# Page loads of the index stage issued in the projection, two key pads placed a stage earlier, and a fifth page slot in the diagonal stage

## What is computed

```
x = layernorm(alpha * x + 0.5 * swiglu(x, ffn1))
a_q, i_q, i_w, q_lat, q_pe, dsa_row, mla_row = project(x)      # row: 64 key, 64 value, 32 index key
# branch A ("dsa"): an index score chooses the 256 best keys (132 for the prompt)
score = sum_h i_w[h] * relu(i_q[h] . k_idx)                    # over the cached keys too
o_a   = softmax(where(chosen, a_q . k / 8, -inf)) @ v
# branch B ("mla"): all keys, through a latent
o_lat = softmax((q_lat . c_kv + q_pe . k_pe) * scale) @ c_kv
x = layernorm(alpha * x + merge(o_a, o_lat) @ w_o)
x = layernorm(alpha * x + 0.5 * swiglu(x, ffn2))
```

## Time and profile before

| | us |
|---|---|
| median of 3 runs | 3232.73 |
| lowest and highest of them | 3229.4, 3234.01 |
| profiled execution | 3235.45 |
| its span, first to last instruction | 3233.7 |
| TensorE busy | 2981.4 (92%) |
| VectorE, ScalarE, GpSimd busy | 1415.6, 1001.1, 641.2 |

### The profile page before, as it was taken

The page is one execution under the profiler, slowest core; times in us unless marked ns, Lnnn a source line. Parts: engine busy times, 40 slices in busy tenths (PEclk is TensorE's granted clock), DMA queues, the critical chain, the costliest instruction groups (busy, mean ns, idle before and its releaser), DMA issues. The chain is left out here.

```text
span 3233.7 us, 45582 instructions
## 1 busy us (share of the span) xinstructions
PE 2981.4 (92%) x18298; PEld 2554.9 (79%) x18298; DVE 1415.6 (44%) x2116; ACT 1001.1 (31%) x1612; POOL 641.2 (20%) x562
## 2 busy tenths in 40 slices
PE   7999999778898889999999999996888988999997
PEld 7999879655576679998799997784656666999975
DVE  2222264468763352222532223644877444322236
ACT  2121233444442232212321222334444433211223
POOL 1111031221122141110221110411302132311103
PEclk9999999889898999999999999997999989999998
DMA  4222452300122332223432224513001233222243
GB/s 117 83 78 78 139 162 63 130 1 1 66 84 95 111 98 78 78 84 131 156 87 83 78 91 144 157 33 131 1 17 66 84 111 129 74 80 82 87 142 126
DMA packets 241737, 293.79 MB, mean 91 GB/s; under 512 B 12624, under 2 KB 205488, under 8 KB 235456
## 3 DMA queue, kind: packets, MB, share of 16 engines
q1 hardware_dynamic: 234688, 229.00, 23.0%
q0 software_dynamic: 6912, 62.92, 5.3%
HBM read 287.72 MB, written 3.88 MB: 90 GB/s over the span
## 5 line engine op out<-in xcount | busy, mean ns | idle before, releaser
L159 DVE TENSOR_TENSOR wlo<-raw,whi 128x1024 fp32r<-128x1024 f32 (+2 forms) x398 | 514.6, 1294 | 1295.4 <-ACT whi L153 1294.3
L153 ACT ACTIVATE whi<-raw 128x1024 fp32r<-128x1024 f32 (+2 forms) x398 | 418.5, 1053 | 1435.7 <-PE ps L608 864.6
L608 PE MATMUL ps<-xth,whi 128*128 128x296 f32 x2624 | 752.1, 299 | 5.4 <-PEq L770 5.4
L608 PE MATMUL ps<-xtl,whi 128*128 128x296 f32 x2624 | 754.6, 300 | 0.0
L608 PE MATMUL ps<-xth,wlo 128*128 128x296 f32 x2624 | 571.7, 300 | 0.0
L608 PEld LDWEIGHTS ps<-xth,whi 128*128 128x128 f32 x2624 | 494.6, 188 | 5.5 <-issue 5.5
L608 PEld LDWEIGHTS ps<-xtl,whi 128*128 128x128 f32 x2624 | 493.3, 188 | 0.0
L608 PEld LDWEIGHTS ps<-xth,wlo 128*128 128x128 f32 x2624 | 427.5, 188 | 0.0
L166 PE MATMUL ps<-whi,hth 128*128 128x512 f32 (+1 forms) x880 | 350.6, 398 | 10.0 <-DVE wlo L159 8.4
L168 PE MATMUL ps<-whi,htl 128*128 128x512 f32 (+1 forms) x880 | 346.9, 394 | 0.0
L167 PE MATMUL ps<-wlo,hth 128*128 128x512 f32 (+1 forms) x880 | 346.8, 394 | 0.0
(11 more groups left out here) (402 smaller groups left out, 4423.2 us busy)
## 6 DMA issues: line engine op xcount, KB each, us to landing
raw<-in_ffn_w_in SPq DMA_DIRECT2D x176, 512.0 KB, 3.8
raw<-in_ffn_w_out SPq DMA_DIRECT2D x176, 512.0 KB, 3.5
raw<-in_w_o SPq DMA_DIRECT2D x32, 512.0 KB, 3.3
raw<-in_w_in SPq DMA_DIRECT2D x16, 507.0 KB, 3.9
gb<-in_ln_g SPq DMA_DIRECT2D x6, 512.0 KB, 5.4
gb<-in_ln_b SPq DMA_DIRECT2D x6, 512.0 KB, 6.3
raw<-in_w_in SPq DMA_DIRECT2D x8, 338.0 KB, 3.9
x<-in_x_prompt SPq DMA_DIRECT2D x1, 1536.0 KB, 10.8
```

Of the source, the lines that this page charges most:

```text
L153: e.activation(dst, T.raw[:, s, 0:width], ACT.Copy).then_inc(S.hi_done, 1)
L159: e.tensor_tensor(w_lo, T.raw[:, s, 0:width], w_hi.bitcast(F32), ALU.subtract).then_inc(S.split_done, 1)
L608: mm = e.matmul(bank(u, up)[:, h, :], part[:, s, w], xp[:, k, o], start=(k == 0 and part is T.whi and xp is T.xth), stop=(k == KD - 1 and ...
```

## The change

Three things are moved or added. *First*, the first two page sets of the index stage are issued in the projection: their places are now fixed where the rounded weights lay (`hi_at`) and behind the keys in `xth`, and GpSimd issues them behind the wait for the last weight, ahead of the `sB` casts. In the index stage `high(0)` and `low(0)` come ahead of the new tokens' relu and score. *Second*, pads 0 and 1 of the prompt stage are cleared and filled at the index stage, by GpSimd at its start and by ScalarE behind its last relu; the prompt stage clears two pads, and TensorE's wait for `pe_keys` is gone. The score at the end of the index stage is copied in halves, bank 4 by VectorE and bank 5 by ScalarE. *Third*, the diagonal stage has a fifth place for a page set, where the score lay; the sets use places 0, 1, 2, 3, 4, 0, 1, 2. Set 4 is issued behind `low(1)` once the bias is set, set `r` from 5 on when the values of request `r - 5` have been used, and `low` trails by one. In that stage ScalarE runs `high(2p + 2)` in slot 4. The latent stage keeps its order. The diff, cut:

```diff
 # proj_tensors
+    T.pads = [... f"pkeys{i}" at T.score_at + 2 * HKEYS * 4 + i * PROMPT * 4 for i in range(2)]
+    T.pg4 = T.M.put("pg4", [P, PAGES, ROW], F32, T.score_at)
+    T.ip1_at = T.xth_at + 3 * PAST * 4
+    T.ip = [T.M.put(f"ip{i}", [P, PAGES, ROW], F32, at) for i, at in enumerate((T.hi_at, T.ip1_at))]
 # proj_stage, gpsimd
                 e.memset(q[:, :, :].bitcast(F32), 0.0).then_inc(S.stack_zero, 1)
+            e.wait_ge(S.w_used, B + NW)
+            for r in range(2):
+                page_load(e, T, r, T.ip[r][:, :, :], W["cache_dsa"], r)
             e.wait_ge(S.sa_done, 2)
 # prompt_block, gpsimd / tensor / scalar / vector
-            for pad in pads:
+            for pad in pads[2:4]:
                 e.memset(pad[:, :], 0.0).then_inc(S.pads_zero, 1)
...
-                    if i == 0:
-                        e.wait_ge(S.pe_keys, 4)
...
-            e.wait_ge(S.pads_zero, 2)
-            for pad, rows in ((pe_keys[0], slice(32, 64)), (pe_keys[1], slice(96, 128))):
-                for dst, src in pad_copy(pad, T.kcT, rows):
-                    e.activation(dst, src, ACT.Copy).then_inc(S.pe_keys, 1)
...
-            e.wait_ge(S.pads_zero, 4)
+            e.wait_ge(S.pads_zero, 2)
...
-            e.wait_ge(S.pe_keys, 4)
             e.wait_ge(S.key_step, 4)
 # page slots
+SLOTS = [[r % 2 for r in range(DEC_B)], [r % 4 for r in range(DEC_B)], [0, 1, 2, 3, 4, 0, 1, 2]]
 # index_block
+    def score_out(e, half, copy):
+        h = PAGES // 2
+        copy(T.score[:, 0:HPAST].rearrange("t (p i) -> t i p", i=PAGES)[:, half * h:(half + 1) * h],
+             T.ps[:, 4 + half, :].rearrange("t (i p) -> t i p", i=h))
 # index_block, gpsimd
-            for r in range(DEC_B):
-                if r >= 2:
-                    e.wait_ge(S.kl_done, r - 1)
+            for pad in pads[0:2]:
+                e.memset(pad[:, :], 0.0).then_inc(S.pads_zero, 1)
+            for r in range(2, DEC_B):
+                e.wait_ge(S.kl_done, r - 1)
                 page_load(e, T, r, ip[r % 2][:, :, :], cache_dsa, r % 2)
 # index_block, scalar
+            high(0)
             e.wait_ge(S.new_dots, 1)
             e.activation(new_relu..., ACT.Relu).then_inc(S.new_relu, 1)
-            high(0)
             high(1)
...
+            e.wait_ge(S.pads_zero, 2)
+            for pad, rows in ((pads[0], slice(32, 64)), (pads[1], slice(96, 128))):
+                for to, of in pad_copy(pad, T.kcT, rows):
+                    e.activation(to, of, ACT.Copy)
+            e.wait_ge(S.weighed, DEC_B // 2)
+            score_out(e, 1, cp)
 # index_block, vector
+            low(0)
             e.wait_ge(S.new_weighed, 1)
...
-            low(0)
             low(1)
...
-            e.tensor_copy(T.score[:, 0:HPAST]..., flat[:, 4 * 512:4 * 512 + HPAST]...)
+            score_out(e, 0, e.tensor_copy)
 # sample_block
+    slots = [T.pg[:, i, :, :] for i in range(4)]
+    if not M:
+        slots.append(T.pg4[:, :, :])
+    pg = [slots[i] for i in SLOTS[1 if M else 2]]
 # sample_block, gpsimd
-            for r in range(1, 4):
-                low(r)
-            for r in range(4, DEC_B):
-                values_done(r // 2 - 2, r % 2)
-                page_load(e, T, r, pg[:, r % 4, :, :], cache, r % 4)
-                low(r)
+            low(1)
+            if not M:
+                e.wait_ge(S.bias_set, 4)
+                pages(4)
+            low(2)
+            low(3)
+            if M:
...
+            else:
+                for r in range(5, DEC_B):
+                    values_done((r - 5) // 2, (r - 5) % 2)
+                    pages(r)
+                    low(r - 1)
+                low(DEC_B - 1)
 # sample_block, scalar
-                    if p + 1 < PAIRS and j == 6:
+                    if p + 1 < PAIRS and j == (6 if M else 4):
                         high(2 * p + 2)
```

More of the change, by code:

```diff
@@ L881, in proj_tensors @@
     T.score_at = A.top + 16384
+    T.pads = [T.M.put(f"pkeys{i}", [P, PROMPT], F32, T.score_at + 2 * HKEYS * 4 + i * PROMPT * 4) for i in range(2)]
+    T.pg4 = T.M.put("pg4", [P, PAGES, ROW], F32, T.score_at)
+    assert T.score_at + PAGES * ROW * 4 <= T.arena + 2 * KF * TOK * 4
     T.sI = T.M.put("sI", [SAMPLE, IH, P], F32R, A.top + 16384)
@@ L1471, in sample_step, with pad_copy @@
         e.match_replace(T.swork[:, :], best, left[:, :], TAKEN).then_inc(S.s_round_done, 1)
+def pad_copy(pad, src, rows):
+    return [(pad[rows, c:c + w], src[rows, k0:k0 + w]) for c, k0, w in ((0, 0, S0), (S0, TAIL, PROMPT - S0))]
 def prompt_block(nc, T, S, next_cache):
@@ L1940, with pages_there @@
 INDEX_SEMS = ["w_zero", "w_set", "kh_done", "kl_done", "turned", "out_act", "out_dve", "dots_done", "relu_done", "weighed",
[L1941 to L1956, removed]
+              "new_dots", "new_relu", "new_weighed", "scored", "pads_zero"]
+PAGE_SEMS = ["page_in0", "page_in1", "page_in2", "page_in3", "page_in4"]
+SLOTS = [[r % 2 for r in range(DEC_B)], [r % 4 for r in range(DEC_B)], [0, 1, 2, 3, 4, 0, 1, 2]]
+def pages_there(e, T, l, stage, r):
+    slot = SLOTS[stage][r]
+    a_layer = sum(slots.count(slot) for slots in SLOTS)
+    before = sum(slots.count(slot) for slots in SLOTS[:stage]) + SLOTS[stage][:r].count(slot)
+    e.wait_ge(T.page_in[slot], l * (16 * a_layer) + 16 * (before + 1))
 def page_load(e, T, r, dst, cache, slot):
@@ L2059, in high @@
             def high(r):
-                pages_there(e, T, l, 0, r % 2, r // 2)
+                pages_there(e, T, l, 0, r)
                 if r >= 2:
@@ L2253, in values_done, with pages @@
                 e.wait_ge(S.v_done, 10 * p + 5 * b + 5)
+            def pages(r):
+                page_load(e, T, r, pg[r], cache, SLOTS[1 if M else 2][r])
             low(0)
             for r in range(1 if M else 2, 4):
-                page_load(e, T, r, pg[:, r, :, :], cache, r)
+                pages(r)
             if M:
@@ L2263, in _ @@
                                 base=0, pattern=[[1, P]], channel_multiplier=-1).then_inc(S.ones_set, 1)
-            for r in range(1, 4):
-                low(r)
-            for r in range(4, DEC_B):
-                values_done(r // 2 - 2, r % 2)
-                page_load(e, T, r, pg[:, r % 4, :, :], cache, r % 4)
-                low(r)
+            low(1)
[5 more added lines that the diff above has]
+            if M:
+                for r in range(4, DEC_B):
+                    values_done(r // 2 - 2, r % 2)
+                    pages(r)
+                    low(r)
+            else:
+                for r in range(5, DEC_B):
+                    values_done((r - 5) // 2, (r - 5) % 2)
+                    pages(r)
+                    low(r - 1)
+                low(DEC_B - 1)
             if M:
@@ L2281, in turn_chunk @@
                     if g == 0:
-                        pages_there(e, T, l, stage, r % 4, r // 4)
+                        pages_there(e, T, l, stage, r)
                     for k in range(4):
-                        mm = e.transpose(bank(("c", ch))[:, k * P:(k + 1) * P], pg[:, r % 4, 4 * g + k, 0:RL], T.ident[:, :])
+                        mm = e.transpose(bank(("c", ch))[:, k * P:(k + 1) * P], pg[r][:, 4 * g + k, 0:RL], T.ident[:, :])
                     mm.then_inc(S.bank_ps, 1)
```

25 lines of the change are left out of this document (10 added, 15 removed).

## The result

The changed kernel takes **3200.89 us** (3195.75 to 3201.28), the kernel before 3232.86 in the same rounds (3229.4 to 3234.01): a ratio of 0.9899 with a 95% interval of 0.9882 to 0.9916. That is 32.0 us less, where 28.5 were forecast. The time lies in the forecast's range of 3196 to 3213, between the forecast of 3204.2 and rival (a), 3198.

What follows compares the result with a forecast made beforehand. TensorE's idle time in the index and diagonal stages was taken as what the change can win: 12.8 + 1.8 + 1.9 + 12.0 = 28.5 us off 3232.73, so 3204.2 us, range 3196 to 3213.

Steps and rivals of the forecast that it cites:

- rival (a): Diagonal-stage boundaries: shorter idle keeps the clock up, up to 1 us more each, 6 in all, 3198 us; chance 15%.
- Part 1, projection: Projection: issuing page sets 0 and 1 there costs 0 us; at worst 0.1 us per layer is lost.
- Part 1, index stage: Index stage: pages already landed, first transpose and relu sooner; 6.8 us layer 1, 6.0 layer 2, 12.8 in all.
- rival (b): Index stage: page 3 late or `high(2)` waits, stall moves on; 3 to 4 us back per layer, 3211 us; 14%.
- the 599.3 of the sum: Index stage of layer 1: forecast start of the first transpose, instead of 605.25, 5.95 us earlier.
- signs of being wrong: Index stage: the sign meant is a wait for a page before `high(2)` or `high(3)` of over 2 us.
- Part 2: Index stage's end: score copy split over VectorE and ScalarE, 0.9 us per layer, 1.8; moved memsets and key copies hidden.
- Parts 2 and 3: Part 2, index stage's end: 1.8 us; Part 3, prompt stage's start, key copies after two memsets instead of four: 1.9 us.
- Part 4: Diagonal stage: fifth place and `high` at slot 4 end boundary waits; 8.5 us layer 1, 3.5 layer 2, 12.0 in all.
- t0: Diagonal stage: moment a pair's last score is out; forecast floor for the next pair's first score matmul is t0 + 2.3.
- (c): Dense stages: less rest lowers the granted clock; over 1.3% eats the gain, 2.5% gives 3260 us; chance 4%.
- (d): Index stage: early-loaded pages not landed, or issues wait for `sA`; fifth place alone left, 3217 us; chance 3%.

Runs made afterwards that it cites:

- the pair of kernels with and without the 14 transposes: Changed kernel with `high` back at slot 6 in the diagonal stage: 3212.4 us; plus 14 identity transposes in TensorE's stall at each of six boundaries: 3206.7 us.
- a third buffer: Changed kernel with three places for pages in the index stage: 3191.6 us (ratio 0.9873).
- the last two kernels: Three-places kernel plus 13 transposes before the last index weighing and 24 before the prompt's keys: 3189.0 us; plus 4 at the index stage's head: 3188.2 us.

## Why the prediction was right, and where it was off

- **Part 1, projection: cost nothing, as said.** The two issues run at 584.49 and 585.99 for 1.19 and 0.94 us, and the `sB` cast starts at 587.22 (before 587.40). The pages had landed by 594.2, before the block began. The rule of the Trainium skill on the shared port (SBUF — State Buffer, "SBUF: two separate sides") made no difference that these durations show.
- **Part 1, index stage: 11.7 us instead of 12.8.** From the stage's start to the first relu 5.3 us were gained in layer 1 and 5.6 in layer 2, and 0.8 more in layer 1 up to the last relu. Against the kernel with Part 1 undone it is 10.5 to 10.8. The term that was off is the landing of set 3: I took its old time of 7.7 us to the new place. But `high(1)` no longer waits for a page of its own, so sets 2 and 3 are issued 1.5 us apart instead of some 3, and share the DMA engines; set 3 took 9.5 and 8.1 us. This is rival (b) in part, at 1.1 us over both layers and not at 3 to 4 each. One of the prediction's own signs of being wrong did appear: `high(3)` waited 3.41 and 2.3 us for its page. The first transposes also came 0.4 us later than the 599.3 of the sum (599.73), by the memsets of Part 2 at the stage's head, which the prediction called hidden.
- **Parts 2 and 3: 3.3 us instead of 3.7,** by the stretch from the last weighing to the first reduction. Near the forecast at that place, but about 0.8 us of it is paid back at the head of the index stage, and the total alone shows nothing.
- **Part 4: the mechanism of the waits was right, the size was not.** The floor at t0 + 2.3 came out as 2.37 at all six boundaries, and the distances from t0 to the scores shrank by 11.5 us (forecast 12.0). The stage gained 17.6. The sum counted the wait and left out the half clock behind it, which I had read off and put into rival (a) at up to 1 us a boundary. From t0 to t0 the six boundaries gained 18.7, so 7.2 lie outside the waits (1.2 each); 1.1 of the 18.7 was lost again behind the last t0 of layer 1. That these 7.2 are the clock is worked out from this difference; what measures the clock is the pair of kernels with and without the 14 transposes, 8.4 us over both layers. My doubt, that an idle stretch of 1.2 us might bring the clock down too, was wrong: the stalls that remain are 1.24 to 1.48 us, and the granted clock behind all six is 1.00. So rival (a) came true beside the forecast, at 7.2 us where it had 6.
- **The match of 11.5 and 12.0 is partly luck.** Some 5 us of both are the page waits of layer 1 in the one execution of before that was traced. With Part 4 undone the same loads landed 2.2 us sooner, the waits came to 6.6, and the stages still took 16.4 us more.
- **The clock rule.** The Trainium skill (TensorE: Matmul & The Clock Gate, "Part 1: The HAM clock gate") has the clock fall after idle time; the trace agrees, 0.50 behind 2.33 us of idle and 1.00 behind 0.69, in two kernels that differ only in the 14 transposes.
- **Rivals (c) and (d)** did not happen: the granted clock in the dense stretch is 0.99 (before 0.98), and ScalarE's waits for sets 0 and 1 went.
- The right total owes something to errors of opposite sign: 1.5 us too much for Parts 1 to 3, 5.6 too little for Part 4.
- Undone one by one, the parts give back 7.7, 16.5 and -0.1 us of total, 24.1 of the 32.0. With some 5 us of uncertainty in each, the runs do not show where the rest belongs.

## What to carry to other kernels

Price a stall of TensorE by the time from one event of the loop to the next, not by the idle time alone: here half of what the boundaries gained in layer 2 (3.6 of 6.9 us) lay outside the waits. When an early load removes a wait, look at which later loads now go out closer together, because that wait had kept them apart; here a third buffer gave 9.3 us, more than the 1.1 that were missing. A change of 3 us in a kernel whose identical stretches differ by up to 3 us has to be read in the trace, at its place. And a wait seen in one trace may not be there in the next: in the diagonal stage the gathers that had no other gather beside them took 6.0 to 9.1 us to land.

## What the runs showed of the hardware that I had not expected

The same idle stretch does not always bring the clock down. Before the last weighing of the index stage TensorE is idle for 1.97 us in the ten kernels that do not fill this stretch; the same eight matmuls then took 3.59 us in layer 1 of the changed kernel and 1.94 in layer 2 (timeline of TensorE):
```profile
646.29 3.59 PE L2038 MATMUL ps<-irelu,wall 128*64 128x512 f32 x8 [1.97 <-ACT irelu L2090]
...
2220.81 1.94 PE L2038 MATMUL ps<-irelu,wall 128*64 128x512 f32 x8 [1.97 <-ACT irelu L2090]
```
Over these ten kernels with two layers each it took 1.94 us eight times and 2.57 to 3.63 us twelve times (before 2.62 and 3.31), and each time that it took more, the clock fell within it. That is up to 1.7 us a layer which no edit made. With the stretch filled (idle 0.55) it took 1.94 in all four cases, layers 1 and 2 of the last two kernels. At the head of the index stage, on the other hand, four more transposes at half clock did not bring the clock back sooner.
